# Root-mean-square norms of nine head chunks: one product with a block matrix of 1/64 and a root by logarithm and exponential, chunk by chunk

## Chip, cores and metric

The kernel runs as one program on 1 NeuronCore of a Trainium2 chip. The metric is the device time of one execution in microseconds (us); lower is better. PE is TensorE, DVE VectorE, ACT ScalarE, POOL GpSimd and SP SyncE, as in the profile.

## What is computed

Two blocks run over 512 tokens of width 1024. The first block is a gated linear recurrence, followed by a sliding-window attention with 16 query heads and 2 key/value heads of width 64. The second block has two attentions, a gated merge and a large feed-forward part. The part that the change touches is the norm over each head (64 values) of the first block's queries and of its key:

```python
def rmsnorm(x, g):
    x32 = x.astype(jnp.float32)
    y = x32 * lax.rsqrt(jnp.mean(x32 * x32, axis=-1, keepdims=True) + EPS)
    return (y * g.astype(jnp.float32)).astype(x.dtype)
...
    q = rmsnorm(q.reshape(bsz, seq, N_Q_HEADS, HEAD_DIM), q_norm_g)
    o = sliding_window_sink_attention(q, k, v, sinks)
```

## The kernel before

All activations lie transposed, 128 channels on the partitions by 512 tokens in the free dimension. Every weight tile of 128x128 is split into a high and a low part, and each tile of a product takes three matmuls of 128x512 (lines 666 to 668, `gemm`). Eight tiles make a unit: SP fetches it (line 533), ACT makes its high part `wh` (line 862), and DVE its low part `wl` (line 1157), about twenty tiles ahead of their use.

Each engine has one list of instructions, which it works off in order. The list is made when the kernel is built: every step is a small generator that yields ticks (one tick is one weight tile on PE) and `merge` sorts all steps of an engine by tick. So a wait inside a step holds up everything that stands behind it in that engine's list, whatever it is.

The products of the first block's attention are chunks of 128 output channels, eight tiles each: `("kv", 0)` is the key, `("bq", 0)` to `("bq", 7)` are the queries, two heads to a chunk. These nine are the head chunks, numbered 0 to 8; `("kv", 1)`, the value, stands behind chunk 4. When a chunk has ended on PE, DVE scales it out of its PSUM bank (`scaled`, line 1219; `heads`). Chunks 0 and 1 end one tile apart, chunks 2 to 4 follow at eight tiles each, and chunks 5 to 8 come after the value. The scores of the attention (`scores`, line 788) begin shortly after chunk 5.

The norm of the head chunks goes in two parts, chunks 0 to 4 and chunks 5 to 8 (`HEADS`, line 492):

- `head_squares` (ACT, line 991) squares each chunk into `sq[i % 2]` after its eviction.
- `head_sums` (PE, line 720) has four matmuls per chunk. The squares are the stationary operand and the 128x2 matrix `hind` the moving one, so the sums of a head land with the tokens on the partitions, two columns for each 128 tokens.
- `head_roots` (ACT, line 998) takes the square root of all sums of a part at once; `head_norm` (DVE, line 1301) the reciprocal.
- `head_spread` (PE, line 730) turns these back with four transposes, ACT copies them to `qr` (line 1004), and for each chunk one product with a 0/1 matrix from `selt` (line 738) spreads the two factors over 128 partitions, in the bank `PV` (bank 7) for chunks 0 to 4 and in bank 2 for chunks 5 to 8.
- `head_norm` (DVE, line 1308) multiplies the chunk by its factor and by the gain. For chunk 0, the key, DVE also makes two half copies (lines 1312 and 1313); PE swaps its halves by a product with `perm` (line 742), and DVE copies two more halves out of that bank (lines 1316 and 1317).

`qr` is zeroed by POOL (line 1574), and `selt` (320 KB) is fetched by SP (line 550). A spread waits until the one before it in the same bank has been read (`qn_done`).

Of the kernel before, what the change touches and what calls it, by code (L numbers as in the profile page):

```python
# [32 lines left out]
for _n, _w in [("ones", 128), ("qs1", 8), ("qs2", 4), ("eps", 1), ("hind", 2), ("ident", 128), ("perm", 128), ("D1", 256),  # L33
               ("D2", 384)]:
    CST[_n] = (CST_N, CST_N + _w)
    CST_N += _w
# [149 lines left out]
def build(nc, xT, wst, par, cst, sel, nbias, out):  # L186
    ctx = ExitStack()
    with ctx:
# [6 lines left out]
        def f32(ap):  # L195
# [45 lines left out]
        selt = sb("selt", [128, 640], F, ph)  # L241
# [7 lines left out]
        qr = sb("qr", [128, S], F, ph)[:, :]  # L249
        hs = sb("hs", [128, NBLK, 16], F, ph)  # L250
# [43 lines left out]
        par_in, cst_in, cst2_in, sel_in = (sem(n) for n in ("par_in", "cst_in", "cst2_in", "sel_in"))  # L294
# [4 lines left out]
        hsum_done, hturn_done, spread_done, perm_done = (sem(n) for n in ("hsum_done", "hturn_done", "spread_done", "perm_done"))  # L299
# [7 lines left out]
        hrt_done, qr_done, v_done, exp_done, es1_done, pta_done, o_done = (  # L307
            sem(n) for n in ("hrt_done", "qr_done", "v_done", "exp_done", "es1_done", "pta_done", "o_done"))
# [8 lines left out]
        hrcp_done, qn_done, ke_done, bias_done, es0_done, es2_done, rd_done, ptd_done = (  # L317
            sem(n) for n in ("hrcp_done", "qn_done", "ke_done", "bias_done", "es0_done", "es2_done", "rd_done", "ptd_done"))
# [4 lines left out]
        zero_in, u0_done, sum_done, b_done, yl_done, zero_done, nrm_done, fin2_done = (  # L323
            sem(n) for n in ("zero_in", "u0_done", "sum_done", "b_done", "yl_done", "zero_done", "nrm_done", "fin2_done"))
# [11 lines left out]
        def drvc(a, b):  # L336
            return drv[:, a:b]
# [153 lines left out]

        HEADS = [(HEAD_U[0:5], bank[PV], 10, head_tick(4) + 5.0), (HEAD_U[5:9], bank[2], 8, head_tick(8) + 5.0)]
# [25 lines left out]
        def _(e):  # L518
# [16 lines left out]
            def starts():  # L535
# [12 lines left out]
                yield end["wa", 0]  # L548
                q.wait_ge(yl_done, 12)
                e.dma_start(selt[:, :], sel).then_inc(sel_in, 16)  # L550
# [21 lines left out]
        def _(e):  # L572
# [137 lines left out]
            def head_sums():  # L710
                for i in range(9):
                    yield head_tick(i) + 4.0
                    q.wait_ge(sq_done, 16 + i + 1)
                    if i == 0:
                        q.wait_ge(rstd_done, 2)
                    hb = bank[PV] if i < 5 else bank[2]
                    j = i if i < 5 else i - 5
                    a = CST["hind"][0]
                    for n in range(NBLK):
                        done = e.matmul(hb[:, 16 * n + 2 * j:16 * n + 2 * j + 2], sq[i % 2][:, blk(n)],  # L720
                                        cstt[:, a:a + 2], start=True, stop=True)
                    done.then_inc(hsum_done, 1)

            def head_spread(part_):
                us, hb, m, t0 = HEADS[part_]
                yield t0 + 3.0
                q.wait_ge(cst2_in, 16)
                q.wait_ge(hrcp_done, part_ + 1)
                for n in range(NBLK):
                    done = e.transpose(hb[0:m, blk(n)], hs[:, n, 0:m], ident)  # L730
                done.then_inc(hturn_done, 1)
                q.wait_ge(sel_in, 16)
                for i in range(len(us)):
                    yield t0 + 6.0 + 2 * i
                    q.wait_ge(qr_done, part_ + 1)
                    q.wait_ge(zero_done, 1)
                    q.wait_ge(qn_done, 5 * part_ + i)
                    e.matmul(hb, selt[:, blk(i)], qr, start=True, stop=True).then_inc(spread_done, 1)  # L738
                    if part_ == 0 and i == 0:
                        yield t0 + 8.5  # L740
                        q.wait_ge(qn_done, 1)
                        e.matmul(bank[TB[0]], C_("perm"), qu[0], start=True, stop=True).then_inc(perm_done, 1)
# [92 lines left out]
            lanes = [warm_up(), gemm(), last_norm(), head_sums(), head_spread(0), head_spread(1), perm_ka(),  # L835
# [10 lines left out]
        def _(e):  # L846
# [112 lines left out]
            def splits(s, j):  # L959
# [13 lines left out]
                elif s == 2 and j < 2:  # L973
                    q.wait_ge(hsum_done, 8 + j)
# [8 lines left out]
            def head_squares():  # L983
                for i in range(9):
                    yield head_tick(i) + 0.8
                    q.wait_ge(ev_done, ev_no(HEAD_CHUNKS[i]))
                    if i < 2:
                        q.wait_ge(sum_done, 11 + i)
                    else:
                        q.wait_ge(hsum_done, i - 1)  # L990
                    e.activation(sq[i % 2], HEAD_U[i], ACT.Square).then_inc(sq_done, 1)

            def head_roots(part_):
                us, hb, m, t0 = HEADS[part_]
                yield t0
                q.wait_ge(hsum_done, (5, 9)[part_])
                q.wait_ge(hturn_done, part_)
                e.activation(hs[:, :, 0:m], hb[:, 0:64].rearrange("p (n h) -> p n h", n=NBLK)[:, :, 0:m], ACT.Sqrt,
                             bias=C_("eps", 0)).then_inc(hrt_done, 1)
                yield t0 + 4.0  # L1000
                q.wait_ge(hturn_done, part_ + 1)
                q.wait_ge(zero_done, 1)
# [792 lines left out]
```

## Time and profile before

| what | value |
|---|---|
| median of 3 runs | 1220.84 us (1219.04 to 1220.86) |
| the profiled execution, its own time | 1220.71 us |
| its span, first to last instruction | 1218.9 us |
| mean granted TensorE clock over the span | 0.992 of full speed |
| busy: PE / DVE / ACT / POOL | 97% / 52% / 43% / 13% |
| instructions | 14435 |

A row of a timeline has start, duration, engine, line, operation, tiles, and in brackets the idle time of the engine before it with the instruction that ended it. A plain float32 matmul of 128x512 has two passes, so one matmul of the program stands as x2; the three matmuls of a weight tile have one pass each. Matmuls are pipelined: the distance between starts tells what one costs, not its duration.

### The profile page before, as it was taken

Reading aid. Unit: us, or ns where it says so; the run is one execution under the profiler, and the core shown is the slowest. Engines: PE = TensorE matmul, PEld = TensorE weight load, DVE = VectorE, ACT = ScalarE, POOL = GpSimd, SP = SyncE. Lnnn points to the kernel's source line nnn. Section 1 sums busy time; section 2 is a strip of 40 time slices with the busy share of each in tenths; the row PEclk is TensorE's granted clock in tenths of the full one; section 3 lists DMA queues with packets and bytes.
Section 4 is the critical chain, followed back from the end, with each engine's and each line's share of the span. In section 5 each row is a group of like instructions: output and inputs, shape, how many; then the busy total and the mean of one; then the engine's idle time right before and its main releaser. Section 6 shows DMA issues by size and latency. Waiting matters only on the chain.

```text
span 1218.9 us, 14435 instructions
## 1 busy us (share of the span) xinstructions
PE 1187.9 (97%) x5374; PEld 888.5 (73%) x5374; DVE 638.1 (52%) x1079; ACT 521.7 (43%) x903; POOL 157.6 (13%) x197
## 2 busy tenths in 40 slices
PE   8999998999999999999999999999999999999995
PEld 5777766777665678766667677887888888888884
DVE  6787877843656665445444444545544232544221
ACT  6657646542464644334434433335443212433222
POOL 2022113210122302012111110003000000000011
PEclk9999998999999999999999999999999999999998
DMA  5322222322111122312122222223233232232211
GB/s 210 105 87 87 87 78 79 125 94 70 52 36 36 51 70 91 99 52 70 62 84 81 87 70 87 87 92 99 89 101 103 87 95 96 87 96 95 87 52 69
DMA packets 29878, 103.08 MB, mean 85 GB/s; under 512 B 3312, under 2 KB 3568, under 8 KB 29808
## 3 DMA queue, kind: packets, MB, share of 16 engines
q1 hardware_dynamic: 29376, 101.37, 25.4%
q8 instruction: 43, 0.70, 0.2%
q10 hardware_dynamic: 432, 0.79, 0.2%
q14 instruction: 27, 0.22, 0.1%
HBM read 100.05 MB, written 2.10 MB: 84 GB/s over the span
## 4 chain that ended last, share of the span: by engine, by line
PE 90%; DVE 4%; ACT 3%; issue 1%; DMA 0%; POOL 0%; SPq 0%; DVEq 0%; ACTq 0%; POOLq 0%
PE ps L666 27%; PE ps L668 26%; PE ps L667 26%; PE ps L788 3%; PE ps L800 2%; PE ps L831 2%; PE ps L825 1%; DVE cc L1264 1%; ACT wh L862 1%; DVE wl L1157 1%; PE ps L720 1%; PE ps L738 1%; DMA xt<-xT 0%; PE ps L687 0%; PE ps L598 0%
## 5 line engine op out<-in xcount | busy, mean ns | idle before, releaser
L666 PE MATMUL ps<-xgh,wh 128*128 128x512 f32 x848 | 355.0, 419 | 3.1 <-DVE wl L1157 2.4
L668 PE MATMUL ps<-xgh,wl 128*128 128x512 f32 x848 | 336.3, 397 | 0.0
L667 PE MATMUL ps<-xgl,wh 128*128 128x512 f32 x848 | 335.3, 395 | 0.0
L1157 DVE TENSOR_TENSOR wl<-raw,wh 128x1024 fp32r<-128x1024 f32 x180 | 230.1, 1280 | 154.7 <-ACT wh L862 154.6
L862 ACT ACTIVATE wh<-raw 128x1024 fp32r<-128x1024 f32 x180 | 188.3, 1048 | 134.4 <-PE ps L668 134.4
L666 PEld LDWEIGHTS ps<-xgh,wh 128*128 128x128 f32 x848 | 159.3, 188 | 75.6 <-issue 44.1
L668 PEld LDWEIGHTS ps<-xgh,wl 128*128 128x128 f32 x848 | 159.2, 188 | 37.5
L667 PEld LDWEIGHTS ps<-xgl,wh 128*128 128x128 f32 x848 | 159.6, 188 | 33.8 <-issue 2.7
L1034 ACT ACTIVATE Pt<-Pt,stat 128x256 f32<-128x256 f32 (+2 forms) x128 | 64.5, 504 | 132.4 <-DVE stat L1367 54.4
L1621 POOL TENSOR_SCALAR Pt<-Pt,stat 128x256 f32<-128x256 f32 (+2 forms) x128 | 71.2, 569 | 339.2 <-DVE stat L1399 247.8
L668 PE MATMUL ps<-fh,wl 128*128 128x512 f32 x256 | 102.1, 399 | 0.0
L667 PE MATMUL ps<-fl,wh 128*128 128x512 f32 x256 | 100.9, 394 | 0.0
L666 PE MATMUL ps<-fh,wh 128*128 128x512 f32 x256 | 100.5, 393 | 0.0
L1098 ACT ACTIVATE f<-rl 128x512 f32<-128x512 f32 x32 | 20.3, 633 | 99.5 <-DVE rl L1524 99.5
L1595 POOL TENSOR_SCALAR ssq<-sq 128x512 f32<-128x512 f32 x4 | 2.6, 656 | 423.9 <-ACT sq L1118 306.3
L667 PEld LDWEIGHTS ps<-fl,wh 128*128 128x128 f32 x256 | 48.1, 188 | 12.6
L666 PEld LDWEIGHTS ps<-fh,wh 128*128 128x128 f32 x256 | 48.1, 188 | 11.4
L668 PEld LDWEIGHTS ps<-fh,wl 128*128 128x128 f32 x256 | 48.0, 188 | 11.1
L1273 DVE TENSOR_TENSOR xt<-ps,xt 128x512 f32<-128x512 f32 x39 | 26.8, 687 | 55.6 <-PE ps L668 55.6
L1598 POOL TENSOR_TENSOR ssq<-ssq,sq 128x512 f32<-128x512 f32 x27 | 37.8, 1401 | 101.8 <-ACT sq L979 69.2
L666 PE MATMUL ps<-yh,wh 128*128 128x512 f32 x96 | 39.4, 411 | 4.6 <-DVE gu L1219 3.7
L1529 DVE TENSOR_TENSOR fl<-f,fh 128x512 fp32r<-128x512 f32 x32 | 22.2, 693 | 40.5 <-ACT fh L1102 40.5
(225 smaller groups left out, 1561.2 us busy)
## 6 DMA issues: line engine op xcount, KB each, us to landing
raw<-wst SPq DMA_DIRECT2D x180, 512.0 KB, 3.5
bst<-nbias SPq DMA_DIRECT2D x8, 256.0 KB, 4.6
xt<-xT SPq DMA_DIRECT2D x3, 512.0 KB, 7.6
outT<-ot SPq DMA_DIRECT2D x6, 256.0 KB, 3.0
raw<-wst SPq DMA_DIRECT2D x2, 256.0 KB, 4.0
outT<-ot ACTq DMA_DIRECT2D x2, 256.0 KB, 2.7
cstt<-cst SPq DMA_DIRECT2D x1, 448.0 KB, 5.6
selt<-sel SPq DMA_DIRECT2D x1, 320.0 KB, 4.0
```

The costliest lines, as they stand in the source:

```text
L666: e.matmul(o, high, a, start=(k == 0), stop=False)
L667: e.matmul(o, high, b, start=False, stop=False)
L668: e.matmul(o, low, a, start=False, stop=stop).then_inc(tile_done, 1)
L788: e.matmul(o[:, 0:128 * job["nk"]], own, seen, start=True, stop=True).then_inc(score_done, 1)
L800: done = e.transpose(bank[TB[t % 2]][:, blk(i)], p_tile(m, i)[0][:, blk(kb)], ident)
L831: done = e.matmul(bank[PV][r, 256 * half:256 * half + 256], v[:, job["k0"] + kb, 64 * g:64 * g + 64], src.rearrange("p (c h t) -> p c h t" ...
L862: e.activation(wh_t[:, u % NHL, :], raw_t[:, u % NRAW, :], ACT.Copy).then_inc(hi_done, 1)
L1034: e.activation(pa, pa, ACT.Exp, scale=-1.0, bias=stat_(m, 0, i, i + 1), accum_out=stat_(m, 1, i, i + 1)).then_inc(exp_done, 1)
L1157: e.tensor_tensor(wl_t[:, u % NHL, :], raw_t[:, u % NRAW, :], f32(wh_t[:, u % NHL, :]), ALU.subtract).then_inc(lo_done, 1)
L1273: e.tensor_tensor(xt[:, j, :], bank[ch.bank[name]], xt[:, j, :], ALU.add).then_inc(ev_done, 1)
L1598: e.tensor_tensor(ssq, ssq, sq[(n0 + j) % 2], ALU.add).then_inc(sum_done, 1)
L1621: e.tensor_scalar(pm, pm, stat_(m, 3, i, i + 1), 1.0, ALU.mult, ALU.mult).then_inc(nrm_done, 1)
```

## The change

The five small steps are replaced by one chain for each chunk. `hones` is a 128x128 matrix with 1/64 where row and column belong to the same head, so one plain float32 product with the squares gives the mean of the squares of each head, already spread over its 64 partitions, in the chunk's bank (`head_bank`). ACT takes the logarithm of that (bias eps) into `sq`, and then exp(-0.5 x) back into the bank; DVE multiplies from there. `hind`, `selt`, `qr`, `hs`, the transposes, the spreads, the reciprocal and the zeroing are gone. A product waits until DVE has read the bank for the chunk before (`qn_done`); the squares of chunk i + 2 wait for `hrq_done` of chunk i instead of for its sums.

```diff
             def head_sums():
                 for i in range(9):
-                    yield head_tick(i) + 4.0
+                    yield head_tick(i) + 2.4
                     q.wait_ge(sq_done, 16 + i + 1)
+                    q.wait_ge(cst2_in, 16)
+                    q.wait_ge(rstd_done, 2)
+                    q.wait_ge(qn_done, i if i != 5 else 0)
+                    e.matmul(head_bank(i), C_("hones"), sq[i % 2], start=True, stop=True).then_inc(hsum_done, 1)
                     if i == 0:
-                        q.wait_ge(rstd_done, 2)
-                    hb = bank[PV] if i < 5 else bank[2]
-                    j = i if i < 5 else i - 5
-                    a = CST["hind"][0]
-                    for n in range(NBLK):
-                        done = e.matmul(hb[:, 16 * n + 2 * j:16 * n + 2 * j + 2], sq[i % 2][:, blk(n)],
-                                        cstt[:, a:a + 2], start=True, stop=True)
-                    done.then_inc(hsum_done, 1)
-
-            def head_spread(part_):
...
+                        yield head_tick(0) + 6.6
                         q.wait_ge(qn_done, 1)
                         e.matmul(bank[TB[0]], C_("perm"), qu[0], start=True, stop=True).then_inc(perm_done, 1)
...
-            def head_roots(part_):
...
+            def head_roots():
+                for i in range(9):
+                    yield head_tick(i) + 3.6
+                    q.wait_ge(hsum_done, i + 1)
+                    e.activation(sq[i % 2], head_bank(i), ACT.Ln, bias=C_("eps", 0)).then_inc(hln_done, 1)
+                    q.wait_ge(hln_done, i + 1)
+                    e.activation(head_bank(i), sq[i % 2], ACT.Exp, scale=-0.5).then_inc(hrq_done, 1)
...
-            def head_norm(part_):
...
+            def head_norm():
+                for i in range(9):
+                    yield head_tick(i) + 5.4
+                    q.wait_ge(hrq_done, i + 1)
+                    q.wait_ge(drv_done, 24)
+                    col = P_("gk") if i == 0 else drvc(GQ8 + i - 1, GQ8 + i)
+                    e.scalar_tensor_tensor(HEAD_U[i], HEAD_U[i], col, head_bank(i), ALU.mult, ALU.mult).then_inc(qn_done, 1)
+                    if i == 0:
                         q.wait_ge(qn_done, 1)
...
-    put("hind", (np.arange(2)[None, :] == i[:, None] // 64) / 64.0)
+    put("hones", (i[:, None] // 64 == i[None, :] // 64) / 64.0)
```

The lists that `merge` makes show where the new steps stand. The rows come without times. Lines are those of each program: 1157 and 1125 are the same `wl`, 1219 and 1187 the same eviction, 862 and 836 the same `wh`.

DVE before, from the evictions of chunks 0 and 1 (`qu`, `q`) to the eviction of chunk 4:

```order
L1219 TENSOR_TENSOR qu<-ps,rstd 128x512 [waits rstd_done,tile_done]
L1219 TENSOR_TENSOR q<-ps,rstd 128x512 [waits tile_done]
L1157 TENSOR_TENSOR wl<-raw,wh 128x1024 [waits hi_done]
L1219 TENSOR_TENSOR q<-ps,rstd 128x512 [waits tile_done]
L1157 TENSOR_TENSOR wl<-raw,wh 128x1024 [waits hi_done]
L1219 TENSOR_TENSOR q<-ps,rstd 128x512 [waits tile_done]
L1157 TENSOR_TENSOR wl<-raw,wh 128x1024 [waits hi_done]
L1219 TENSOR_TENSOR q<-ps,rstd 128x512 [waits tile_done]
```

DVE in the change, from the eviction of chunk 1 on (the `scalar_tensor_tensor` of line 1271 is the multiplication by the factor):

```order
L1187 TENSOR_TENSOR q<-ps,rstd 128x512 [waits tile_done]
L1271 SCALAR_TENSOR_TENSOR qu<-qu,part,ps 128x512 [waits drv_done,hrq_done]
L1274 COPY ke<-qu 64x512 [waits qn_done]
L1275 COPY ke<-qu 64x512
L1125 TENSOR_TENSOR wl<-raw,wh 128x1024 [waits hi_done]
L1278 COPY ke<-ps 64x512 [waits perm_done]
L1279 COPY ke<-ps 64x512
L1271 SCALAR_TENSOR_TENSOR q<-q,drv,ps 128x512 [waits hrq_done]
L1187 TENSOR_TENSOR q<-ps,rstd 128x512 [waits tile_done]
L1271 SCALAR_TENSOR_TENSOR q<-q,drv,ps 128x512 [waits hrq_done]
L1125 TENSOR_TENSOR wl<-raw,wh 128x1024 [waits hi_done]
L1187 TENSOR_TENSOR q<-ps,rstd 128x512 [waits tile_done]
```

The multiplication of chunk 1, and the four copies of the key, now stand ahead of the eviction of chunk 2; from there on each chunk's multiplication and a `wl` stand ahead of the next chunk's eviction.

ACT before, from the squares of chunks 0 and 1 to the squares of chunk 3:

```order
L991 ACTIVATE sq<-qu 128x512 [waits sum_done,ev_done]
L991 ACTIVATE sq<-q 128x512 [waits sum_done,ev_done]
L862 ACTIVATE wh<-raw 128x1024 [waits tile_done,raw_in1]
L991 ACTIVATE sq<-q 128x512 [waits hsum_done,ev_done]
L862 ACTIVATE wh<-raw 128x1024 [waits tile_done,raw_in2]
L991 ACTIVATE sq<-q 128x512 [waits hsum_done,ev_done]
```

ACT in the change, from the squares of chunk 1 to the squares of chunk 2:

```order
L965 ACTIVATE sq<-q 128x512 [waits sum_done,ev_done]
L971 ACT_TABLE_LOAD
L971 ACTIVATE sq<-ps,cstt 128x512 [waits hsum_done]
L973 ACT_TABLE_LOAD
L973 ACTIVATE ps<-sq 128x512 [waits hln_done]
L971 ACT_TABLE_LOAD
L971 ACTIVATE sq<-ps,cstt 128x512 [waits hsum_done]
L973 ACT_TABLE_LOAD
L973 ACTIVATE ps<-sq 128x512 [waits hln_done]
L836 ACTIVATE wh<-raw 128x1024 [waits tile_done,raw_in1]
L965 ACTIVATE sq<-q 128x512 [waits hrq_done,ev_done]
```

Each logarithm and each exponential has a table load of its own in front of it, and the `wh` that followed the squares of chunk 1 now follows the exponential of chunk 1.

PE in the change, around the product with `perm` (line 716); line 712 is the product with `hones`, here that of chunk 1:

```order
L660 MATMUL ps<-xgh,wh 128x512
L661 MATMUL ps<-xgl,wh 128x512
L662 MATMUL ps<-xgh,wl 128x512
L716 MATMUL ps<-qu,cstt 128x512 [waits qn_done]
L712 MATMUL ps<-sq,cstt 128x512 [waits sq_done]
```

The product with `perm` stood behind the first spread before; now it stands twelve weight matmuls behind the product of chunk 0, and chunk 1's product directly behind it. Fifteen weight matmuls follow until the product of chunk 2, and twenty-four between those of chunks 2, 3 and 4.

## Rows read from the trace of the kernel before

**Rows 1.** The page: busy time by engine, and the chain that ended last.

```profile
PE 1187.9 (97%) x5374; PEld 888.5 (73%) x5374; DVE 638.1 (52%) x1079; ACT 521.7 (43%) x903; POOL 157.6 (13%) x197
...
PE 90%; DVE 4%; ACT 3%; issue 1%; DMA 0%; POOL 0%; SPq 0%; DVEq 0%; ACTq 0%; POOLq 0%
```

**Rows 2.** Groups of instructions on PE, 262 to 450 us: busy us, mean ns.

```profile
L720 PE MATMUL ps<-cstt,sq 128*128 128x2 f32 x72 | 8.5, 240 | 0.0
```

**Rows 3.** Timeline of PE, 272 to 308 us.

```profile
272.90 0.95 PE L720 MATMUL ps<-cstt,sq 128*128 128x2 f32 x8
...
274.02 0.39 PE L667 MATMUL ps<-xgl,wh 128*128 128x512 f32 x1
...
276.32 0.40 PE L667 MATMUL ps<-xgl,wh 128*128 128x512 f32 x1
...
280.52 0.40 PE L667 MATMUL ps<-xgl,wh 128*128 128x512 f32 x1
...
297.65 0.60 PE L730 MATMUL ps<-cstt,hs 128*10 128x128 f32 x4
...
298.32 0.40 PE L667 MATMUL ps<-xgl,wh 128*128 128x512 f32 x1
...
300.65 1.02 PE L738 MATMUL ps<-qr,selt 128*128 128x512 f32 x2
...
301.74 0.41 PE L667 MATMUL ps<-xgl,wh 128*128 128x512 f32 x1
...
306.77 1.13 PE L738 MATMUL ps<-qr,selt 128*128 128x512 f32 x2 [0.59 <-DVE q L1308]
```

**Rows 4.** Whom PE waited for, 262 to 450 us: total us, times, longest.

```profile
PE ps L788 <- DVE stat L1367: 2.3, 2, 1.4
PE ps L788 <- DVE q L1308: 0.9, 1, 0.9
...
PE ps L738 <- DVE q L1308: 0.6, 1, 0.6
```

**Rows 5.** Timeline of ACT: the norm of the layer's input, then a head's squares.

```profile
264.70 0.69 ACT L890 ACTIVATE rstd<-ps,cstt 128x512 f32<-128x512 f32 x1 [2.92 <-PE ps L687]
265.41 1.28 ACT L892 ACT_TABLE_LOAD   x1
266.70 0.64 ACT L892 ACTIVATE rstd<-rstd 128x512 f32<-128x512 f32 x1
267.24 1.04 ACT L862 ACTIVATE wh<-raw 128x1024 fp32r<-128x1024 f32 x1
270.33 0.63 ACT L991 ACTIVATE sq<-qu 128x512 f32<-128x512 f32 x1 [2.04 <-DVE qu L1219]
```

**Rows 6.** Timeline of DVE: eviction of chunk 1, `wl`, a multiplication, a key copy.

```profile
270.30 0.69 DVE L1219 TENSOR_TENSOR q<-ps,rstd 128x512 f32<-128x512 f32 x1
272.64 1.23 DVE L1157 TENSOR_TENSOR wl<-raw,wh 128x1024 fp32r<-128x1024 f32 x1 [1.65 <-ACT wh L862]
...
301.71 0.75 DVE L1308 SCALAR_TENSOR_TENSOR qu<-qu,part,ps 128x512 f32<-128x512 f32 x1 [3.80 <-PE ps L738]
...
304.54 0.68 DVE L1316 COPY ke<-ps 64x512 f32<-64x512 f32 x1
```

**Rows 7.** Timeline of ACT: the second part's root between two exponentials.

```profile
350.04 1.28 ACT L998 ACT_TABLE_LOAD   x1
351.34 0.29 ACT L998 ACTIVATE hs<-ps,cstt 128x32 f32<-128x32 f32 x1
351.64 1.28 ACT L1034 ACT_TABLE_LOAD   x1
```

**Rows 8.** Timeline of PE: the longest wait of this execution.

```profile
186.81 0.80 PE L666 MATMUL ps<-yh,wh 128*128 128x512 f32 x1 [3.73 <-DVE gu L1219]
```

**Rows 9.** Stretches: length, busy us of each engine, granted clock, DMA share.

```profile
188.00:192.00 4.00, 4.00 (x11) 3.14 (x10) 3.05 (x4) 3.36 (x6) 1.29 (x1) 0.50 0.24 98
...
527.00:530.00 3.00, 1.62 (x9) 0.85 (x7) 2.53 (x8) 1.17 (x5) 1.90 (x2) 1.00 0.00 0
```

More of the change, by code:

```diff
@@ L32 @@
 CST_N = 0
-for _n, _w in [("ones", 128), ("qs1", 8), ("qs2", 4), ("eps", 1), ("hind", 2), ("ident", 128), ("perm", 128), ("D1", 256),
+for _n, _w in [("ones", 128), ("qs1", 8), ("qs2", 4), ("eps", 1), ("ident", 128), ("hones", 128), ("perm", 128), ("D1", 256),
                ("D2", 384)]:
@@ L183, in gemm_plan, with build @@
     return ch
-def build(nc, xT, wst, par, cst, sel, nbias, out):
+def build(nc, xT, wst, par, cst, nbias, out):
     ctx = ExitStack()
@@ L293, in build @@
         x_in = [sem(f"x_in{i}") for i in range(5)]
-        par_in, cst_in, cst2_in, sel_in = (sem(n) for n in ("par_in", "cst_in", "cst2_in", "sel_in"))
+        par_in, cst_in, cst2_in = (sem(n) for n in ("par_in", "cst_in", "cst2_in"))
         bias_in = [sem(f"bias_in{i}") for i in range(4)]
@@ L306, in build @@
                              "c_done", "yh_done"))
-        hrt_done, qr_done, v_done, exp_done, es1_done, pta_done, o_done = (
-            sem(n) for n in ("hrt_done", "qr_done", "v_done", "exp_done", "es1_done", "pta_done", "o_done"))
+        hln_done, hrq_done, v_done, exp_done, es1_done, pta_done, o_done = (
+            sem(n) for n in ("hln_done", "hrq_done", "v_done", "exp_done", "es1_done", "pta_done", "o_done"))
         rstd8_done, y2h_done, gt_done, mh_done, fsq_done, fh_done, xf_done = (
@@ L321, in build @@
                              "ml_done", "fl_done", "fin_done"))
-        zero_in, u0_done, sum_done, b_done, yl_done, zero_done, nrm_done, fin2_done = (
-            sem(n) for n in ("zero_in", "u0_done", "sum_done", "b_done", "yl_done", "zero_done", "nrm_done", "fin2_done"))
+        zero_in, u0_done, sum_done, b_done, yl_done, nrm_done, fin2_done = (
+            sem(n) for n in ("zero_in", "u0_done", "sum_done", "b_done", "yl_done", "nrm_done", "fin2_done"))
         def P_(n, i=None, j=None):
@@ L489, in head_tick, with head_bank @@
             return ev_at[HEAD_CHUNKS[i]]
-        HEADS = [(HEAD_U[0:5], bank[PV], 10, head_tick(4) + 5.0), (HEAD_U[5:9], bank[2], 8, head_tick(8) + 5.0)]
+        def head_bank(i):
+            return bank[PV if i < 5 else 2]
         SUMS = {1: "wa", 2: "wb", 3: "wc"}
@@ L989, in head_squares @@
                     else:
-                        q.wait_ge(hsum_done, i - 1)
+                        q.wait_ge(hrq_done, i - 1)
                     e.activation(sq[i % 2], HEAD_U[i], ACT.Square).then_inc(sq_done, 1)
-            def head_roots(part_):
[L994 to L1002, printed above, removed]
-                q.wait_ge(spread_done, 5 * part_)
-                e.activation(qr[0:m, :], hb[0:m, :], ACT.Copy).then_inc(qr_done, 1)
+            def head_roots():
[5 more added lines that the diff above has]
+                    e.activation(head_bank(i), sq[i % 2], ACT.Exp, scale=-0.5).then_inc(hrq_done, 1)
             def copy_v(n, dst, src, tick):
@@ L1570, in zeros @@
                     e.memset(u[:, 0:3], 0.0).then_inc(u0_done, 1)
-                yield end["kv", 0]
-                q.wait_ge(tile_done, A_END)
-                q.wait_ge(sum_done, 12)
-                e.memset(qr, 0.0).then_inc(zero_done, 1)
             def first_sums():
@@ L1784 @@
         "cst": constants(),
-        "sel": np.concatenate([i[:, None] == 2 * c + i[None, :] // 64 for c in range(5)], axis=1).astype(np.float32),
         "nbias": neighbour_bias(a["rpb_2"][0]),
```

57 lines of the change are left out of this document (10 added, 47 removed).

## The prediction

> **What bounds the kernel now.** I read the page first: PE is busy for 97% of the span and makes 90% of the chain that ended last, while ACT is busy for 43% and DVE for 52% [rows 1]. So time on ACT or DVE costs nothing by itself. It costs when PE reaches a matmul whose operand or bank is not ready. Second, I read PE's timeline through the head chunks. A weight matmul starts every 0.233 us (18 of them lie between 276.32 and 280.52), and anything else that PE runs adds its own time to that beat [rows 3]. Third, PE's waits from 262 to 450 us: few and short, 1.5 us for the multiplications of head chunks and 2.3 us for the scores' bias step (the reader is to see that the present order leaves PE almost without a wait) [rows 4]. The question is therefore what the change takes from PE's own work, and which new waits PE gets.
>
> **PE's own work.** The four small matmuls of a chunk's sums go: from 272.90 the next weight matmul but one starts at 274.02, 1.12 us, where 0.23 would do without them, so 0.89 us a chunk, 8.0 us for nine; the 72 rows of that line are these nine chunks, eight each [rows 2, 3]. The transposes go, 298.32 - 297.65 - 0.23 = 0.44 us for each of the two parts, 0.9 us [rows 3]. The nine spreads go at 301.74 - 300.65 - 0.23 = 0.86 us each, and nine products with `hones` come, of the same shape and type, so at the same 0.86 us: nothing [rows 3]. `perm` only moves. Together -8.9 us. The waits on the multiplications go as well, 0.6 and 0.9 us; by the starts around 306.77 the first cost 0.9 rather than 0.6, so I take 2.0 for the two: -2.0 us [rows 3, 4].
>
> **Off PE.** The reciprocals, the copies to `qr`, the zeroing on POOL and the `selt` transfer of 320 KB go; no wait of PE names them, so they are worth nothing. The constants' second transfer grows by 64 KB and lands over 250 us before its first use: nothing. The multiplications on DVE remain nine of 0.75 us [rows 6].
>
> **The new chain on ACT.** The layer's norm shows its length: logarithm 0.69, a table load 1.28, exponential 0.64, each starting when the one before is nearly through, and then `wh` 1.04 [rows 5]. From the list, each of the nine chunks has this, with a second load ahead of the logarithm: 1.28 + 0.60 + 1.28 + 0.53 = 3.7 us of ACT, 33 us in all. ACT has room for it; the waits are what count. I walk the lists with these durations, and with the 1.3 us from the start of a plain product to its last column (1.02 us, and the 0.24 us of weight load ahead).
>
> *Chunk 0.* Its squares start at 270.33 and those of chunk 1 at 271.03 [rows 5, 6]. The load runs from 271.6 to 272.9, the logarithm to 273.5, the load to 274.7, the exponential to 275.4, DVE's multiplication to 276.2 [rows 5, 6]. PE stands at `perm` at 271.3 + 0.86 + 12 x 0.233 = 274.9. It waits **1.3 us**.
>
> *Chunks 1 and 2.* Chunk 1's product is queued behind `perm`: 276.2 + 0.86 = 277.1, landed 278.3. The logarithm follows with its load already done, then load and exponential: 280.8. Behind that stand `wh` to 281.8 and, on DVE, `wl` (1.13), two key copies out of the bank (0.7 each), the multiplication of chunk 1 (0.65), and only then the eviction of chunk 2 (0.7), though it was ready long before: 285.8 [rows 5, 6]. Its squares end at 286.4 and its product starts at 286.5. PE has only 0.86 + 15 x 0.233 = 4.4 us of work from 277.1 on and stands there at 281.4. It waits **5.1 us**. This is the dearest step.
>
> *Chunks 3 and 4.* Now a loop holds: product landed 1.3, logarithm 0.6, load 1.28, exponential 0.65, multiplication 0.65 (beside it `wh`, so `wl` follows 0.3 later), `wl` 1.13, eviction 0.7, squares 0.7, in sum 7.3 us. PE's beat is 24 x 0.233 + 0.86 = 6.5 us. It waits **0.9 us** each time, and 0.2 us more before the value's transposes. First stretch: 1.3 + 5.1 + 0.9 + 0.9 + 0.2 = 8.4 us.
>
> *The clock.* Idle for 3.73 us at 183 us, PE ran at 0.50 of full speed from 186.8 to 192.1 (its 1.2 GHz level); the 12 matmuls in it took 5.3 us where 2.8 would do, so 2.5 us were lost [rows 8, 9]. A wait of 1.4 us at 528 left the clock at 1.00 [rows 9]. The new wait of 5.1 us is longer than the first, so I count 2.5 us again; but chunk 3's product waits 0.9 us at its end anyway, which this slow stretch swallows. Net +1.6.
>
> *Chunks 5 to 8* lie among the scores, where PE, DVE, ACT and POOL hand each softmax on. Chunk 5's multiplication holds the first bias step on DVE: 1.6 us. Chunk 6's 3.7 us, with a `wh` behind, stand ahead of the eighth exponential, and the transposes that need it come 2.6 us late. Chunk 7's do the same to a product (1.4) and to a score (0.6), chunk 8's to a product (0.9). That is 7.1 us. The lower bound is nothing: the old root's block of 1.28 + 0.29 + 1.28 = 2.85 us at 350.04 cost PE no wait [rows 4, 7]. The upper bound is all four blocks in full, 4 x 3.7 = 14.8 us. I take 7 because each block is 0.85 us longer than the one that was hidden and three of the four have a `wh` of 1.04 queued behind them [rows 5, 7].
>
> **The sum.** -8.9 - 2.0 + 8.4 + 1.6 + 7.0 = +6.1 us. Small waits of a few tenths that the present order has in the same stretch and the new one shifts are worth some 0.3 less. The profiled execution took 1220.7 us, 0.1 us under the median of the runs shown, so **1226.5 us**, 0.47% slower.
>
> **A rule against the rows.** The Trainium skill, "ScalarE: Activation LUTs", section "Table sets: the hidden batching unit", says that a logarithm followed by an exponential takes one load, since one set holds both. Here a load of 1.28 us stands between line 890's logarithm and line 892's exponential all four times, and the list of the change has one ahead of each of its logarithms and exponentials [rows 5]. The rows decide; the rule's result is the third rival. The same page, section "What ACT_TABLE_LOAD costs", adds a drain and states about 2.66 us for a switch. In the rows the exponential starts 1.29 us after its load began and the load follows the logarithm at once, so no drain shows [rows 5]. By the page's figure each of the 18 loads would cost 1.38 us more, an estimate of up to 25 us above mine.
>
> **Rivals.** *First, about the same (0.12):* the blocks among the scores are hidden as the old one was [rows 7], so 7 becomes 1 to 3, or the clock stays up. 6.1 - 4 to 6 gives 1221 to 1223. For it: DVE and ACT are half idle; against it: four blocks instead of one, with `wh` behind. *Second, slower still (0.16):* the clock falls once more after the wait of 2.6 us among the scores. Whether such a wait is enough, the waits of 3.73 and 1.4 us leave open [rows 8, 9]. That adds 2.5, or the waits pass on: 1229 to 1233. *Third, faster (0.04):* logarithm and exponential need no load between them. The loop is then 7.3 - 1.28 = 6.0 us, under PE's 6.5, so chunks 3 and 4 wait for nothing, and chunk 1's `perm` neither; chunk 2's wait, with one load less on its chain, is 3.8 us and may still bring the clock down (2.5); the scores' share falls to 1 or so: -8.9 - 2.0 + 3.8 + 2.5 + 1 = -3.6, so 1217. It decides at a loop of 6.5 us, that is when 0.9 us are saved. *Fourth, faster (0.05):* the lists hold PE less than I think, because evictions are not held up behind the multiplications; then only the work counts, 1220.7 - 8.9 - 2.0 + 2 = 1212. Against it stands the order on DVE. My forecast keeps 0.63, between 1223.5 and 1229.
>
> **The numbers.** 0.2% of this time is 2.4 us, about what a measurement of this kernel can tell from no change. Slower by more: 0.63 + 0.16 = 0.79, and a little of the first rival's upper edge makes 0.80. Within it: 0.11. Faster: 0.09. The range takes the forecast's own, most of the first rival and the near half of the second: 1222 to 1231.
>
> **What would show it.** Right: line 712 waits for ACT's squares about 5 us near 281 us, and the clock reads 0.50 behind it; 18 table loads of 1.28 us at lines 971 and 973; the multiplications of line 1271 idle some 4.6 us on ACT before each of chunks 2 to 4; products of line 712 at 0.86 us each; and waits of lines 788, 800 and 831 between 315 and 365 us. Wrong: fewer loads; no wait at chunk 2's product; a clock of 1.00 throughout; or PE's beat unbroken from 277 to 310 us.

## The result and the profile after

| | time, us | ratio to the kernel before (95%) |
|---|---|---|
| before, beside the change | 1220.84 median (1218.85 to 1221.13, 5 runs) | |
| the change | 1228.32 median (1226.58 to 1228.79, 5 runs) | 1.0061 [1.0048, 1.0073] |
| its profiled execution | 1228.3, span 1226.5, clock 0.987 | |

The change makes the kernel slower by 0.61%, 7.5 us. The forecast was 1226.5, with a range of 1222 to 1231. Four of the five executions took 1228.2 to 1228.8 us at a mean clock of 0.987 or 0.988, the profiled one among them, and the fifth took 1226.6 us at 0.991, so what is said below of the clock is the account of the commoner kind. The line numbers are 6 to 42 lower than before: 666 to 668 are now 660 to 662, 788 is 762, 800 is 774, 831 is 805, 862 is 836, 1157 is 1125, 1219 is 1187, 1308 is 1271, 1367 is 1329 and 1621 is 1579. The products with `hones` are line 712. In the experiments an edit moves a line by up to 12 more (762 is 763, 765 or 766 in some, 712 is 715 or 716).

From the page of the changed kernel, the same two lines as in [rows 1], busy time by engine and the chain that ended last:

```profile
PE 1183.5 (96%) x5294; PEld 881.1 (72%) x5294; DVE 636.9 (52%) x1077; ACT 549.9 (45%) x931; POOL 157.1 (13%) x196
...
PE 89%; DVE 4%; ACT 4%; issue 2%; DMA 1%; SPq 0%; POOL 0%; DVEq 0%; ACTq 0%; POOLq 0%
```

PE is busy for 4.4 us less, half-clock stretches included, yet the span is 7.6 us longer. ACT has 28 us more to do. That is still only 45%, so nothing in this line tells why. The waits tell it: whom PE waited for between 255 and 450 us in the changed kernel (total us, times, longest), to be held against [rows 4].

```profile
PE ps L712 <- ACT sq L965: 5.4, 2, 4.8
PE ps L762 <- DVE stat L1329: 4.4, 5, 1.4
PE ps L774 <- POOL Pt L1579: 2.7, 2, 2.2
PE ps L805 <- ACT PT L1020: 1.2, 1, 1.2
PE ps L716 <- DVE qu L1271: 1.1, 1, 1.1
PE ps L805 <- ACT q L1030: 0.9, 1, 0.9
```

These are 15.7 us of waits, where the kernel before had 4.6 us. PE's timeline in the changed kernel shows where the three in the first stretch fall, and the first two weight matmuls behind the long one:

```profile
275.00 0.40 PE L662 MATMUL ps<-xgh,wl 128*128 128x512 f32 x1
276.47 1.12 PE L716 MATMUL ps<-qu,cstt 128*128 128x512 f32 x2 [1.08 <-DVE qu L1271]
...
281.57 0.40 PE L662 MATMUL ps<-xgh,wl 128*128 128x512 f32 x1
286.75 2.08 PE L712 MATMUL ps<-sq,cstt 128*128 128x512 f32 x2 [4.78 <-ACT sq L965]
287.83 1.42 PE L660 MATMUL ps<-xgh,wh 128*128 128x512 f32 x1
289.05 0.63 PE L661 MATMUL ps<-xgl,wh 128*128 128x512 f32 x1
...
302.49 1.13 PE L712 MATMUL ps<-sq,cstt 128*128 128x512 f32 x2 [0.58 <-ACT sq L965]
```

After the last weight matmul at 281.57, the next start would be due at 281.80. It comes at 286.75, so 4.95 us are lost where the row shows 4.78 us of idle time. Behind it the weight matmuls take 0.63 us instead of 0.40 and start every 0.43 us instead of every 0.233. The windows of the changed kernel (length, busy us of the engines, granted clock, DMA share, GB/s) show why, and that the clock falls a second time among the scores:

```profile
282.00:286.00 4.00, 0.00 (x0) 0.00 (x0) 3.83 (x5) 0.07 (x1) 0.00 (x0) 0.76 0.39 114
288.00:290.00 2.00, 2.00 (x5) 1.20 (x5) 0.00 (x0) 1.12 (x2) 0.00 (x0) 0.50 0.00 0
290.00:292.00 2.00, 2.00 (x8) 1.59 (x7) 0.50 (x1) 1.99 (x3) 0.00 (x0) 0.77 0.00 0
...
336.00:338.00 2.00, 2.00 (x6) 1.01 (x6) 1.57 (x4) 0.81 (x4) 0.70 (x2) 0.50 0.10 14
```

By the means of the first and the third window, 0.76 and 0.77, the clock fell near 284.1, while PE stood idle, and rose near 290.9. What the long wait waits for is read from the two lists beside it. ACT in the changed kernel:

```profile
279.20 1.28 ACT L973 ACT_TABLE_LOAD   x1
280.49 0.60 ACT L973 ACTIVATE ps<-sq 128x512 f32<-128x512 f32 x1
281.03 1.04 ACT L836 ACTIVATE wh<-raw 128x1024 fp32r<-128x1024 f32 x1
286.06 0.63 ACT L965 ACTIVATE sq<-q 128x512 f32<-128x512 f32 x1 [3.99 <-DVE q L1187]
```

DVE in the changed kernel, in the same microseconds:

```profile
282.11 1.23 DVE L1125 TENSOR_TENSOR wl<-raw,wh 128x1024 fp32r<-128x1024 f32 x1 [4.78 <-ACT wh L836]
283.25 0.68 DVE L1278 COPY ke<-ps 64x512 f32<-64x512 f32 x1
283.95 0.69 DVE L1279 COPY ke<-ps 64x512 f32<-64x512 f32 x1
284.68 0.75 DVE L1271 SCALAR_TENSOR_TENSOR q<-q,drv,ps 128x512 f32<-128x512 f32 x1
285.35 0.68 DVE L1187 TENSOR_TENSOR q<-ps,rstd 128x512 f32<-128x512 f32 x1
```

Read backwards from 286.75: the product waits for the squares of 286.06, these for the eviction of 285.35. The eviction could have run about 2 us ahead of the time at which the product was due: in e6 below, where nothing holds it, it starts at 279.82 and the product at 281.91. Here it stands behind four instructions on DVE, the first of which (`wl`) waits for `wh`, and `wh` stands behind Exp on ACT. The loads are there, nine on each of the two lines (groups of instructions on ACT: count, busy us, mean ns):

```profile
L971 ACT ACT_TABLE_LOAD x9 | 11.5, 1283 | 0.2
L973 ACT ACT_TABLE_LOAD x9 | 11.5, 1283 | 0.2
```

### The profile page after: what moved, and what is told of

Read it like the earlier page. It is cut to its first block, busy times and chain, and to the rows that moved or that the text cites. A ratio compares the mean times of both kernels' runs of the same rounds, so it can differ in the third digit from the quotient of the medians.

```text
span 1226.5 us, 14302 instructions
## 1 busy us (share of the span) xinstructions
PE 1183.5 (96%) x5294; PEld 881.1 (72%) x5294; DVE 636.9 (52%) x1077; ACT 549.9 (45%) x931; POOL 157.1 (13%) x196
## 4 chain that ended last, share of the span: by engine, by line
PE 89%; DVE 4%; ACT 4%; issue 2%; DMA 1%; SPq 0%; POOL 0%; DVEq 0%; ACTq 0%; POOLq 0%
PE ps L660 27%; PE ps L662 26%; PE ps L661 26%; PE ps L762 3%; PE ps L774 2%; PE ps L805 2%; ACT wh L836 1%; DVE wl L1125 1%; PE ps L799 1%; PE ps L712 1%; DMA xt<-xT 1%; ACT Pt L1003 0%; DVE cc L1232 0%; PE ps L592 0%; PE ps L681 0%
```

## The experiments

Ten kernels in three groups; each group shared a chip with runs of the kernel before. One thing is measured throughout: by how much the last weight matmul starts later or earlier than in the kernel before ("at the end"), by the two timelines. For the change it is +7.6 us. Each kernel has one trace, and a part of this number can arise ahead of the head chunks, where nothing was changed: at 262 us the weight matmuls already start 1.6 us later in e1, 1.3 earlier in e2, 0.6 later in e9 and 1.5 later in e10; in the others it is at most 0.3.

**e1, no logarithm.** The logarithm is left out in all nine chunks.

```
-  e.activation(sq[i % 2], head_bank(i), ACT.Ln, bias=C_("eps", 0))
+  e.activation(sq[i % 2], head_bank(i), ACT.Copy)
```

> All nine logarithms are plain copies of the sums, so the logarithm is left out of the computation; the instruction lists stay as they are, and no table load stands between the steps on ScalarE any more. My theory: the loads are in the loop eviction, squares, product, Ln, Exp, multiplication, next eviction, and make it 7.3 us long where PE's beat is 6.5 us. Without them chunk 2's product still waits 3 to 4 us, since the order of VectorE's list is unchanged, chunks 3 and 4 wait for nothing, chunk 6's block among the scores loses its waits of 2.2 us on the normalised probabilities and of 1.3 us on their transposed copies. Walking the lists with the rows' durations gives 9.4 us less than the changed kernel: 1217 to 1220 us. Rival A, the loads run beside other work and only the order of the lists costs: within 2 us of the changed kernel, 1226 to 1229 us. Rival B, the loads are all of the loss: below the kernel before by all of PE's saved work, 1212 us or less, and no wait of over 1 us at line 712.

Measured: 1214.24 us (1213.86 to 1217.23), ratio 0.9962 [0.9949, 0.9975]. PE's waits in e1, 255 to 450 us, but for one of 0.4 us:

```profile
PE ps L712 <- ACT sq L965: 3.4, 1, 3.4
PE ps L762 <- DVE stat L1329: 2.5, 3, 1.4
...
```

The logarithm's instruction stays, as a copy of 0.60 us instead of 0.69, so nearly all that goes is the loads. Both rivals fall. Without loads 12 us come back (1.0061 - 0.9962 of 1220), so they were not beside other work. But a wait of 3.4 us at chunk 2's product stays, so they are not all of it. Chunks 3 and 4 and the scores go as expected. The median lies 3 us below my band, the profiled execution (1217.2) within it; that one also had a half-clock stretch near 220 us, ahead of the heads, which the change doesn't touch.

**e2, multiplications behind the next eviction.**

```
-                    yield head_tick(i) + 5.4
+                    yield head_tick(i) + (5.4 if i == 0 else 9.2)
```

> The multiplications of chunks 1 to 8 stand behind the next chunk's eviction on VectorE instead of ahead of it (tick +9.2 instead of +5.4), the second pair of key copies in a list of its own. My theory: that an eviction is queued behind a multiplication that waits for Exp is only one half of the loop; the product of the next chunk also waits for this multiplication, because the five chunks share one bank, so the product of chunk 2 still waits about 4 us (5.1 us forecast before, 4.8 us in the profile), those of chunks 3 and 4 up to 1 us: 1226 to 1229 us, 0 to 2 us below the changed kernel. Rival: the order on VectorE alone makes the wait; then the wait of chunk 2's product falls under 1 us and the time to 1221 to 1223 us.

Measured: 1228.33 us (1226.07 to 1232.71), ratio 1.0073 [1.005, 1.0095]; wait of chunk 2's product 4.2 us. By the starts from 262 us on, this trace is 0.9 us quicker than the change's. As I expected in size, but not for my reason. DVE's list in e2, the two key copies between these rows left out:

```profile
280.74 1.23 DVE L1125 TENSOR_TENSOR wl<-raw,wh 128x1024 fp32r<-128x1024 f32 x1 [4.78 <-ACT wh L836]
...
283.31 0.69 DVE L1187 TENSOR_TENSOR q<-ps,rstd 128x512 f32<-128x512 f32 x1
```

The eviction is ahead of the multiplication now and still late, because `wl` and two copies are ahead of it, and `wl` waits for ACT. The shared bank, which I had named, isn't what holds it.

**e3, PE kept busy in the wait.** Five products that nobody reads.

```
+                    if i == 2:
+                        for _ in range(5):
+                            e.matmul(bank[TB[1]], C_("hones"), cstt[:, a:a + 512], start=True, stop=True)
```

> Five products of the block matrix with constants, read by nobody, run on PE ahead of chunk 2's product, where it waited 4.8 us. They add no work behind that wait as long as five of them take no longer than it (5 x 0.86 = 4.3 us at the full clock). My theory: half the clock behind that wait comes from PE's standing idle; with PE kept busy the granted clock stays 1.00 between 286 and 291 us, and what half the clock costs there (1.6 us forecast) comes back: 1226 to 1227.5 us, 1 to 2 us below the changed kernel. Rival A: the clock falls there for another reason (the chip's budget, since PE does more work now), and it is 0.5 for some us within the next 20 us all the same, with the time unchanged or up to 2 us longer. Rival B: the clock's fall is hidden by the waits behind it (chunk 3's product waits for its squares anyway): clock 1.00, and a wait of about 1 us at chunk 3's product in its place, the time within 0.7 us of the changed kernel.

Measured: 1227.71 us (1226.12 to 1230.09), ratio 1.0065 [1.0048, 1.0081]: no different from the change. Windows of e3:

```profile
288.00:290.00 2.00, 2.00 (x11) 1.59 (x9) 0.00 (x0) 1.97 (x3) 0.00 (x0) 1.00 0.00 0
...
324.00:328.00 4.00, 4.00 (x14) 2.86 (x14) 1.80 (x9) 1.19 (x6) 1.27 (x4) 0.50 0.00 0
```

PE in e3 at the first scores:

```profile
320.87 0.49 PE L766 MATMUL ps<-ke,q 64*128 64x128 f32 x4 [1.34 <-DVE stat L1333]
```

The half clock at 288 us is gone, so PE's standing idle had made it. By the starts the change lost 2.0 us to it: chunk 2's product starts at 286.75 in the change and at 286.70 in e3, and the seventh weight matmul behind it at 291.07 and at 289.07. Of this 0.95 were given back at chunk 3's product, which in e3 waits 0.7 us for its squares (rival B's part). The products of chunks 2, 3 and 4 start 7.42 and 7.41 us apart in e3, which is the loop that I had put at 7.3. But in this execution the clock fell at 321.7 us for 6.8 us, behind the wait of 1.34 us above, where the change at the same place had the same wait, then one of 0.87 us, and kept its clock. That cost e3 2.0 us against the change. So neither my theory nor rival A holds in full: the fall has a cause in the wait, and taking that wait away doesn't spare PE the next one.

**e4, spaced order.** The same instructions; both lists are rearranged and chunk 1 is moved away from chunk 0. The three pairs are the ticks of the product, of Ln and Exp, and of the multiplication; the permutation and its key copies get lists of their own, at +9.0 and +10.5.

```
-                    yield head_tick(i) + 2.4
+                    yield head_tick(0) + 7 if i == 1 else head_tick(i) + 2.4
-                    yield head_tick(i) + 3.6
+                    yield head_tick(0) + 8.2 if i == 1 else head_tick(i) + (3.6 if i == 0 else 4.2)
-                    yield head_tick(i) + 5.4
+                    yield head_tick(0) + 10.2 if i == 1 else head_tick(i) + (5.4 if i == 0 else 6.2)
```

> The same instructions as in the changed kernel, in another order: Ln and Exp of a chunk behind the high part of the next weights' split on ScalarE (tick +4.2), its multiplication behind the low part on VectorE but ahead of the next eviction (+6.2), chunk 1's product, Ln and Exp and multiplication 4.6 ticks later than in the changed kernel, the permutation and its key copies in lists of their own. My theory: nothing in the change but the order makes PE wait; nine products cost PE what nine spreads did, and the saved nine groups of sums and two of transposes (8.9 us) come through. Walking the lists gives waits of 0.5 us in the first stretch, clock 1.00 throughout, and among the scores 0.7, 1.2 and 0.8 us: 1211 to 1215 us, 14 us below the changed kernel and 6 to 9 us below the kernel before. Rival A: the chain squares, product, Ln, Exp, multiplication with its two loads is too long for PE's beat whatever the order, waits of 1 us or more come back at chunks 2 to 4 and the time is 1219 to 1224 us. Rival B: the product of the block matrix costs PE more than the 0.86 us of its row (what stands before it on PE is lengthened): 1216 to 1219 us with no wait at it.

Measured: 1212.18 us (1211.44 to 1213.13), ratio 0.9934 [0.9918, 0.9951]; at the end -7.8 us. PE's waits in e4 from 255 to 450 us (two more, of 0.4 and 0.2 us, are left out):

```profile
PE ps L763 <- DVE stat L1335: 3.0, 4, 1.4
PE ps L806 <- ACT PT L1021: 0.5, 1, 0.5
PE ps L712 <- DVE qu L1275: 0.5, 1, 0.5
...
```

With those, 4.6 us of waits, as much as the kernel before. This is the same arithmetic with the same 18 loads, 16 us faster than the change and 8 us faster than the kernel before. Both rivals fall: the chain with its loads fits PE's beat, and the product costs no more than its row. It is also the time that the prediction's fourth rival gave, 1212, for lists in which no eviction is held up; that rival was wrong of the change's order and right of this one.

**e5, Ln and Exp behind `wh`, alone.**

```
-                    yield head_tick(i) + 3.6
+                    yield head_tick(i) + (3.6 if i == 0 else 4.2)
```

> One number changed: Ln and Exp of chunks 1 to 8 stand behind the high part of the next weights' split on ScalarE (tick +4.2 instead of +3.6); VectorE's list stays as in the changed kernel. My theory: the wait of chunk 2's product has two causes in a row, the split on ScalarE behind Exp and the next eviction on VectorE behind a multiplication that waits for Exp. With the first alone taken away the wait of chunk 2's product falls from 4.8 us to 1 to 2 us, but now the products of chunks 3 and 4 wait as long (the loop through the multiplication is still longer than PE's beat), and among the scores 1.7 us come at two or three blocks: 1222 to 1225 us, 4 to 6 us below the changed kernel, still not below the kernel before. Rival A, the order on ScalarE alone was the cause: 1211 to 1215 us. Rival B, it changes nothing because VectorE holds the eviction all the same: 1226 to 1229 us.

Measured: 1226.68 us (1222.84 to 1227.85, 7 runs), ratio 1.0042 [1.0027, 1.0056]. PE's waits in e5, 255 to 450 us, and DVE where chunk 3 is evicted:

```profile
PE ps L762 <- DVE stat L1329: 7.4, 7, 1.7
PE ps L712 <- ACT sq L965: 3.9, 3, 1.3
```

```profile
288.16 0.75 DVE L1271 SCALAR_TENSOR_TENSOR q<-q,drv,ps 128x512 f32<-128x512 f32 x1 [5.56 <-ACT ps L973]
...
289.96 0.68 DVE L1187 TENSOR_TENSOR q<-ps,rstd 128x512 f32<-128x512 f32 x1
```

The long wait has become three of 1.25, 1.31 and 1.30 us, as expected: the eviction now stands behind a multiplication that idles for Exp. The median is 1.7 us above my band. The profiled execution had its clock at 0.50 from 322 to 328 us and lowered again between 352 and 356 us (0.57), which I had not counted; its bias steps waited 7.4 us in all, more than walked.

**e6, both moves.** e5's and e2's edits together, chunk 1 at its old place.

> Both moves together, and chunk 1 left at its place: Ln and Exp behind the split on ScalarE (+4.2), the multiplications behind the next eviction on VectorE (+9.2). The move on VectorE alone gave nothing (run e2). My theory: the two waits stand in a row in one loop, so that only both moves free it; walking the lists gives no wait at the products of chunks 2 to 4, 1.2 us at the permutation near 276 us, 1.1 and 0.8 us among the scores, clock 1.00: 1211 to 1214 us, the same as the spaced order (e4). Rival A, the gain of e4 came from moving chunk 1 away from chunk 0 (both use one bank), which is not done here: 1217 us or more, with a wait of over 3 us at a product. Rival B, each move has its own share: the sum of e2 and e5.

Measured: 1212.34 us (1212.18 to 1212.81), ratio 0.9931 [0.9917, 0.9946]; at the end -8.4 us. PE's waits in e6, 255 to 450 us, but for one of 0.5 us; 4.6 us with it:

```profile
PE ps L762 <- DVE stat L1334: 2.5, 3, 1.4
PE ps L716 <- DVE qu L1274: 1.1, 1, 1.1
PE ps L805 <- ACT PT L1020: 0.5, 1, 0.5
...
```

Alone, e2's move changed the ratio by +0.0012 and e5's by -0.0019; together they change it by -0.0130. Neither of the first two is clear of the noise, since the intervals of e2 and e5 overlap that of the change. That is two causes in a row in one loop: whichever is left still holds the eviction. Rival A falls, since chunk 1 was not moved, and so does rival B, the sum of the two.

**e7, no logarithm among the scores.** It is left out (e1's copy in its place) in chunks 5 to 8 alone.

> The logarithm is left out for the last four chunks alone (a copy in its place, so no table load), chunks 0 to 4 as in the changed kernel. My theory: the eight loads among the scores are what puts 7 us of waits there (2.2 us on the normalised probabilities near 334 us and the half clock behind it, 1.2 us on transposed copies near 351 us, 0.9 us near 366 us); without them 6 to 8 us come back there and the first stretch keeps its 4.8 us wait: 1219 to 1222 us. Rival A, PE has the waits in the scores because the first stretch made ScalarE late, not for the loads: less than 2 us come back, 1226 to 1229 us. Rival B, the half clock alone is the loss there: 2 us come back.

Measured: 1219.54 us (1218.24 to 1221.83, 10 runs), ratio 0.9993 [0.9983, 1.0003]; at the end -0.9 us. PE's waits in e7, 255 to 450 us (1.1 us at `perm` and 0.4 us at the transposes left out):

```profile
PE ps L712 <- ACT sq L965: 5.4, 2, 4.8
PE ps L762 <- DVE stat L1332: 2.5, 3, 1.4
...
```

The first stretch keeps its 4.8 us, and every new wait among the scores is gone. The loads of the last four chunks cost 8.5 us at the end (7.6 + 0.9). Both rivals fall.

**e8 and e9, a quicker product.** Squares rounded to float32r, in tiles of their own; e8 on the order of e4, e9 on that of e6.

```
+        honr = sb("honr", [128, 128], R, ph)[:, :]
+        sqr = [sb(f"sqr{i}", [128, S], R, ph)[:, :] for i in range(2)]
...
-                    e.activation(sq[i % 2], HEAD_U[i], ACT.Square)
+                    e.activation(sqr[i % 2], HEAD_U[i], ACT.Square)
...
-                    e.matmul(head_bank(i), C_("hones"), sq[i % 2], start=True, stop=True)
+                    e.matmul(head_bank(i), honr, sqr[i % 2], start=True, stop=True)
```

> The spaced order of e4, with the squares of the nine chunks written as float32r into tiles of their own and the block matrix copied to float32r once, so that a product takes one pass instead of four. My theory: PE bounds this version (waits of 2 to 3 us in all are left), so that PE's saved time comes through in full: 9 products of 0.86 us fall to the 0.23 us that a 128x512 float32r product takes in the rows of the weight products, 5.6 us less than e4: 1205 to 1208 us. Rival A, the chain of the next step (Ln, Exp, multiplication, eviction) sets the beat as soon as PE is quicker: waits of 0.5 us come up at each product and the time is 1209 to 1212 us. Rival B, a product right behind float32r products was hidden in part anyway, and nothing changes by more than 1 us.

> Both moves of e6 and the float32r products of e8 together. In e8 the products saved their 5 us, but the product of a chunk stood 0.5 to 1.1 us behind the square or the multiplication of the chunk before, and half the clock came near 316 us. My theory: these waits come from the place of the multiplications ahead of the eviction (which e6 has not); here the products of chunks 1 to 4 wait for nothing, waits of 1.9 us are left at the permutation near 276 us and of 1.2 us at two blocks of the scores, and what the products save comes through but for these: 1207 to 1210 us if the clock stays up, 1209 to 1212 us with one stretch of half the clock in the scores. Rival A: with quicker products something else sets the beat (ScalarE, with two loads to a chunk): waits of 0.5 us and more at the products, 1211 to 1213 us, as e8. Rival B: a product's saved passes were never on the path: the time of e6, 1212 us, with no waits.

Measured: e8 1212.74 us (1211.43 to 1213.82), ratio 0.9934 [0.9918, 0.9949]; e9 1208.46 us (1206.82 to 1209.16), ratio 0.9902 [0.9887, 0.9917]. PE in e8:

```profile
281.46 0.47 PE L715 MATMUL ps<-sqr,honr 128*128 128x512 f32 x1 [0.75 <-DVE q L1281]
...
294.96 0.49 PE L715 MATMUL ps<-sqr,honr 128*128 128x512 f32 x1 [0.81 <-ACT sqr L972]
```

In e8 the 0.6 us that a product saved came back as a wait at the next one. By the starts e8 is 0.85 us ahead of e4 when the scores begin, where six products could have saved 3.8. Then a longer wait at the first bias step and a clock of 0.50 from 315 to 321.8 us cost 2.6 us. So the waits are rival A's, and its time is missed by 0.7 us; the clock is a second loss beside them. With the multiplications behind the eviction (e9), PE's waits in 255 to 450 us are these and one of 0.4 us:

```profile
PE ps L765 <- DVE stat L1340: 2.6, 3, 1.4
PE ps L719 <- DVE qu L1280: 1.7, 1, 1.7
PE ps L808 <- ACT PT L1026: 1.1, 1, 1.1
...
```

No product waits, as the theory of e9 had it, and 3.5 us more come off against e6 (at the end -11.9). So e8's rival A was a matter of the order too, and its reading that ScalarE sets the beat falls. e9 is the fastest version of this study, 1% under the kernel before.

**e10, e6 with chunk 1 moved away as well.**

> e6 with the product of chunk 1, its Ln and Exp 4.6 ticks later and the permutation and its copies in lists of their own, as in e4, so that only the wait of 1.1 us at the permutation near 276 us should go: 0.5 us is left there. My theory: 0.6 to 0.9 us below e6, 1210.5 to 1212 us, since PE bounds this stretch. Rival: the wait comes back at the first block of the scores, whose bias is added by VectorE, and the time is that of e6 (1212 to 1213 us).

Measured: 1211.88 us (1210.12 to 1213.23, 5 runs), ratio 0.9933 [0.992, 0.9945]. The wait at `perm` is replaced by one of 0.5 us at chunk 1's product, but the medians can't be told apart: 0.6 us is under what they resolve. The timelines can tell. e10's weight matmuls start 1.53 us later than e6's ahead of the heads, because e10's clock was at 0.50 from 218.6 to 222.0 us, and 0.93 to 0.95 us later from chunk 2's product to the end. So 0.6 us are gained in the first stretch, and the rival's wait at the scores doesn't come (0.86 us there, 0.87 in e6). This rests on one trace of each.

## Why the prediction was right

It was right in sign and within its range, and the mechanism is the one it named. That the number is within 2 us owes something to terms that cancel, as the end of this section shows. Step by step:

**PE's own work, -8.9, and two waits, -2.0.** e6 has as long waits as the kernel before (4.6 us each, 255 to 450 us) and starts its last weight matmul 8.4 us earlier. So the work saved is about 8.4 us: right but for 0.5. The product and the spread do cost the same (in the change 272.65 - 271.56 - 0.23 = 0.86). The two waits on the multiplications of query chunks are gone, as forecast, from the list of the change and from that of e6; but in e6 others of the same sum stand in their place.

**Chunk 0, 1.3.** The row shows 1.08 us idle. By the starts it is 276.47 - 275.00 - 0.23 = 1.24. Right.

**Chunk 2, 5.1, "the dearest step".** 4.95 by the starts. Right, also in its cause, as a chain: e2 and e5 each undo one link and gain little, e6 undoes both and the wait is gone. The text named the multiplication first, and thought of `wl` and the copies as what it stood among. By e2 they weigh as much.

**Chunks 3 and 4, 0.9 each.** Chunk 4's product waits 0.58 us by its row, about 0.8 by the starts. Chunk 3's waits for nothing, since half the clock had used up its 0.9, as forecast. The walk's 1.3 us from a product's start to the logarithm was too long (1.06 in the change, 277.43 to 278.49), and its other steps a little short: the loop took 7.4 us in e3 instead of 7.3.

**The clock, +1.6 net in this stretch and nothing later.** This is the term that was mis-sized. The stretch at half the clock lasted from 284.1 to 290.9 us, as long as the one before at 185.7 to 192.5, but 2.7 us of it passed while PE stood idle anyway, so 4.2 us of PE's work fell into it instead of 5.3. By e3 it cost 2.0 us instead of 2.5, of which 1.0 stayed. But the clock fell again at 335.3 us, behind the wait of 2.2 us. There weight matmuls start later by 1.5 us more than the same ones in e7. That is the second rival's mechanism, with a smaller price than its 2.5, and it had been given 0.16. Together 2.5 us stayed instead of 1.6.

**Among the scores, +7.0.** Each step can be read by holding the starts of the same weight matmuls of the change against those of e7:

| where in the change | forecast | measured |
|---|---|---|
| bias step held by chunk 5's multiplication, 322 us | 1.6 | 1.4 |
| transposes behind chunk 6's block, 334.6 us | 2.6 | 2.5 |
| half the clock behind them | 0 | 1.5 |
| product, then bias step, behind chunk 7's block, 351 and 353.5 us | 1.4 + 0.6 | 1.3 + 0.6 |
| product behind chunk 8's block, 365.6 us | 0.9 | 1.0 |
| sum | 7.1 | 8.3 |

ACT in the change shows chunk 6's block, with the exponential that the transposes wait for at its end:

```profile
329.62 0.69 ACT L971 ACTIVATE sq<-ps,cstt 128x512 f32<-128x512 f32 x1
330.32 1.28 ACT L973 ACT_TABLE_LOAD   x1
331.62 0.60 ACT L973 ACTIVATE ps<-sq 128x512 f32<-128x512 f32 x1
332.15 1.04 ACT L836 ACTIVATE wh<-raw 128x1024 fp32r<-128x1024 f32 x1
333.10 0.39 ACT L1003 ACTIVATE Pt<-Pt,stat 128x128 f32<-128x128 f32 x1
```

The lower bound of this term, nothing, was in reach all the same: e6 has the same eight loads among the scores, in another order, and PE's waits are those of the kernel before.

**The sum.** The measured delay of +7.6 splits by two experiments: -8.4 for e6, 7.5 between e6 and e7, 8.5 between e7 and the change. The forecast was +5.8 (6.1 less 0.3 for small waits), 1.8 short, and the second fall of the clock cost 1.5. The other terms are off as well and nearly cancel, which is luck: work, small waits and chunk 0 together -8.4 instead of -9.9, the loop of chunks 1 to 4 with its clock 7.5 instead of 8.7. The split isn't sharper than some 0.3 us, since e7's half clock behind the long wait lasted 3.4 us and the change's 6.8.

**The rule on the tables.** The Trainium skill, "ScalarE: Activation LUTs", section "Table sets: the hidden batching unit", would have logarithm and exponential share one load. The change has nine loads ahead of each, so the third rival had no ground. e1 shows what the rival would have been worth with no load at all: 1214 us. The drain of the section "What ACT_TABLE_LOAD costs" doesn't show either: in the rows of chunk 6's block the load at 330.32 follows the logarithm's end at 330.31, and the exponential starts 1.30 us after it.

## What to carry to other kernels

Where every engine works off one list in order, an instruction that waits holds all that stands behind it. A chain of five small steps on ACT and DVE was harmless or cost 16 us depending only on whether `wh`, `wl` and the eviction that PE needs next stood ahead of Ln, Exp and the multiplication or behind them. Put what feeds the bounding engine first and the longer chain behind it. Look for two such links in one loop before giving up an order: undoing either alone gained nothing that the runs could tell here, both together 16 us. Last, before spending a saving on the bounding engine, see that nothing waits at the point where it is made: e8's was lost in waits and to the clock behind one of them, the same edit in e9 was worth 3.5 us.

## What the runs showed that was not expected

**The clock's falls move.** In the change the clock fell during the wait of 4.78 us and stayed at 0.50 for 6.8 us. In e7, with a wait of 4.79 us at the same product, it stood at 1.00 to the end of the wait and fell at 287.3 us, for 3.4 us. Where no wait at that product was longer than 1.3 us (e3, e5, e8), the clock fell at the first scores instead, for 6.8 us each time, 0.8 to 2.0 us after the end of waits of 1.34, 1.69 and 1.20 us. In the change, and in e2, waits of 1.34 and 0.87 us at the same place left it at 1.00. The waits of 2.2 us further on brought a fall of 3.4 us in the change, in e2 and in e3. e4, e6 and e9, with at most 0.93 us at the first scores, had none among the heads and scores, though e9 had waited 1.74 us at `perm` at 277 us. So the length of a wait alone doesn't decide it, and what does these runs don't settle. A window of e8:

```profile
316.00:320.00 4.00, 4.00 (x14) 2.86 (x14) 1.90 (x10) 1.32 (x6) 1.13 (x4) 0.50 0.00 0
```

**A wait costs more than its row.** The idle time begins at the last column of the matmul before. The next start was due 0.17 us earlier (281.80 against 281.97 in the rows of the change), and the product behind a wait takes 1.12 or 1.13 us instead of 1.02. So a wait at one of these products costs PE some 0.27 us more than its row shows. The forecast had counted by starts, which is why its terms hold and the rows look smaller.
